# Expert slots by rank, wide and narrow in turns, and four weight pieces of the first expert in places of their own

## The chip, the cores and the metric

The kernel runs on one NeuronCore of one Trainium2 chip. The metric is the device time of one execution in microseconds (us). Engines are named as in the profile: PE is TensorE, DVE VectorE, ACT ScalarE, POOL GpSimd, and SP the SyncE queue, which issues the weight transfers.

## The reference

Two decoder blocks run one after the other on 256 tokens of width 1024, all in fp32, each with two layers of attention and feed-forward networks. The change touches one part: the second layer of the first block has, where the first layer has a dense network, a mixture of eight experts. Each token goes to its two best experts, and each expert is a gated network of width 3584:

```python
def _swiglu(x, w1, w3, w2):
    return (jax.nn.silu(x @ w1) * (x @ w3)) @ w2

def _moe(x, w_router, w1, w3, w2):
    ...
    logits = (xt @ w_router).astype(jnp.float32)
    top_v, top_e = lax.top_k(logits, TOP_K)          # TOP_K = 2, N_EXPERTS = 8
    gates = jax.nn.softmax(top_v, axis=-1)
    ...
    yb = lax.map(run, (buf.reshape(n_blocks, EXPERT_BLOCK, D), block_e)).reshape(P, D)
    y = jnp.zeros((T, D), x.dtype).at[stok].add(yb[dest] * sg[:, None].astype(x.dtype))
```

256 tokens with two experts each make 512 pairs, 64 per expert on average. For the inputs that `setup_inputs()` draws, the eight experts get 64, 73, 69, 66, 78, 76, 45 and 41 tokens.

## The kernel before

**Weights.** The weights of one expert (w1, w3 and w2, 42 MB) lie in DRAM as 28 pieces of 128 columns of its hidden width. A piece is 1536 KB, 12 KB in each of the 128 partitions: w1, w3 and w2 of these columns, a third each. The weight ring in SBUF (`weight_ring`) has room for eight pieces in this stage; seven places are used (`ROUND` = 7, `expert_unit(q)` gives place q), the eighth is empty. An expert is computed in four rounds of seven pieces (`ROUNDS` = 4).

**SP.** SP waits until PE has used up the piece in a place and then issues the next transfer into it (`load_expert`; `expert_used` counts used pieces over the whole stage). All weight transfers go through SP's one queue in program order. The first seven pieces are issued while the stage before still computes, as soon as the ring's places come free. Which expert comes first is fixed (expert 0), so that its weights can be fetched before the router has decided; the others come in order of falling token count, read from `expert_order`.

**Slots.** Each expert works on a fixed number of token slots. PE gathers the tokens into slots by a product with a 0/1 matrix (`gather`). The widths go by position in the order (`TIERS`): the first expert 88, the second 96, the other six 80, together 664. If an expert has more tokens than its position has slots, all engines take the other branch (`If(most <= CAP)`), in which each expert works on all 256 tokens.

**PE.** For a piece, `chosen_up` makes the two products with w1 and w3 and `chosen_down` the one with w2. The weights are the stationary operand and the slots the moving one; the 128 output columns are split into two strips of 64 (`GROUPS`), which run beside one another in the array. In the profile one piece is 64 matmuls at L844 (up) and 32 at L854 (down). `expert_rounds` puts down(q-1) behind up(q): a round is up 0, up 1, down 0, up 2, down 1 and so on to up 6, down 5, down 6. ACT (silu, L1448) and DVE (product, L1875) work between up and down of a piece. When an expert is done, `expert_result` turns its rows around (L861, L866) and scatters them to the tokens (L876); in the first expert the next one's gather (L819) stands between L866 and L876, in the others behind L876.

**Code.** Each of the three tiers has code of its own on PE, ACT and DVE, and the six experts of the last tier run through the same code in a loop. A round is a loop too: one pass of it holds 672 matmuls and as many weight loads.

The positions are made on DVE (L2245 to L2262): `places` is each expert's rank by token count, expert 0 always first, and comparing it with the numbers 0 to 7 gives the order.

## Time and profile before

| | us |
|---|---|
| median of three runs | 3165.56 (3163.49 to 3168.33) |
| span of the profiled execution | 3164.2 |
| expert stage, first product of the first expert to last product of the last | 859.4 to 1705.1 |
| PE busy, whole span | 3109.1 (98%) |
| transfers of expert pieces | 224 of 1536 KB |

The profiled execution's own time is its span, 3164.2 us; the median lies 1.4 us above it. The eight experts begin at 859.4, 972.4, 1093.5, 1199.1, 1301.3, 1403.5, 1506.7 and 1610.0 us. A window over one expert shows what each engine was busy with and how fast the weights came in; the chain of work shows when each round began, and where a transfer stands in the chain, PE waited for it. A busy PE is not by itself the limit: weights that come late stretch the same work.

### The profile page before, as it was taken

The numbers are of one execution on the slowest core, as the hardware profiler recorded it, in microseconds if no ns is written. First come the engines' busy times: TensorE is split into PE (matmuls) and PEld (weight loads), VectorE is DVE, ScalarE is ACT, GpSimd is POOL, SyncE is SP. The second block draws the span as 40 slices with busy tenths as digits, with TensorE's granted clock in tenths as the row PEclk, the third lists the DMA queues.
The fourth block names the chain that finished last, engine by engine and source line by source line (L and its number), as shares of the span: only waits on it lengthen the run. The fifth ranks groups of instructions, "written<-read, shape, count | busy, mean of one in ns | idle before, by whom it ended". The sixth has DMA issues, their size and how long they took to land.

```text
span 3164.2 us, 79565 instructions
## 1 busy us (share of the span) xinstructions
PE 3109.1 (98%) x36280; PEld 2651.8 (84%) x36280; DVE 1330.7 (42%) x2668; ACT 398.3 (13%) x1040; POOL 53.6 (2%) x86
## 2 busy tenths in 40 slices
PE   9999999999999999999998999999999999999998
PEld 6686894978599999999998976999895976999894
DVE  2252566543201101111013565654566575655465
ACT  1240000042110000000001001111100001121100
POOL 0000000000000000000000000000000000000000
PEclk9999999999999999999999999999999999999999
DMA  7434443433499999999997444434444444534442
GB/s 257 145 111 159 160 173 142 175 133 117 198 411 365 364 418 421 426 426 426 427 426 316 172 167 159 175 134 160 160 160 169 164 170 156 188 120 163 154 176 86
DMA packets 63109, 714.37 MB, mean 226 GB/s; under 512 B 7568, under 2 KB 9232, under 8 KB 11888
## 3 DMA queue, kind: packets, MB, share of 16 engines
q1 hardware_dynamic: 59328, 703.62, 56.5%
q0 software_dynamic: 1008, 5.94, 0.5%
q10 hardware_dynamic: 2624, 2.65, 0.4%
q8 instruction: 114, 1.87, 0.2%
q14 instruction: 35, 0.29, 0.0%
HBM read 709.30 MB, written 1.05 MB: 224 GB/s over the span
## 4 chain that ended last, share of the span: by engine, by line
PE 94%; DMA 2%; DVE 2%; ACT 1%; issue 1%; POOL 0%; SPq 0%; POOLq 0%; DVEq 0%; ACTq 0%
PE psum L653 50%; PE psum L844 15%; PE psum L774 10%; PE psum L854 8%; PE psum L912 5%; DMA weight_ring<-in_experts 2%; PE psum L1256 1%; PE psum L876 1%; PE psum L819 1%; PE psum L691 1%; PE psum L687 1%; PE psum L983 1%; PE psum L686 0%; PE psum L1230 0%; POOL statistics L575 0%
## 5 line engine op out<-in xcount | busy, mean ns | idle before, releaser
L653 PE MATMUL psum<-arena,weight_ring 128*128 128x128 f32 (+1 forms) x6752 | 938.7, 299 | 5.1 <-issue 3.2
L653 PEld LDWEIGHTS psum<-arena,weight_ring 128*128 128x128 f32 x6752 | 881.8, 192 | 49.1 <-issue 11.1
L844 PE MATMUL psum<-arena,weight_ring 128*64 128x80 f32 (+2 forms) x14336 | 553.4, 235 | 7.8 <-ACT arena L1461 6.4
L844 PEld LDWEIGHTS psum<-arena,weight_ring 128*64 128x64 f32 x14336 | 532.2, 137 | 11.6 <-ACT arena L1461 6.4
L653 PE MATMUL psum<-weight_ring,arena 128*128 128x128 f32 (+4 forms) x3264 | 494.8, 309 | 2.7 <-DVE arena L2069 2.7
L653 PEld LDWEIGHTS psum<-weight_ring,arena 128*128 128x128 f32 x3264 | 431.7, 192 | 55.2 <-issue 34.2
L1875 DVE TENSOR_TENSOR arena<-arena,psum 128x80 f32<-128x80 f32 (+2 forms) x224 | 54.0, 241 | 716.6 <-ACT arena L1448 716.6
L854 PE MATMUL psum<-arena,weight_ring 128*64 128x80 f32 (+2 forms) x7168 | 296.5, 235 | 5.4 <-issue 5.3
L854 PEld LDWEIGHTS psum<-arena,weight_ring 128*64 128x64 f32 x7168 | 276.5, 137 | 6.4 <-issue 6.4
L912 PE MATMUL psum<-weight_ring,arena 128*128 128x512 f32 x384 | 166.9, 593 | 0.0
L912 PEld LDWEIGHTS psum<-weight_ring,arena 128*128 128x128 f32 x384 | 72.3, 190 | 86.1 <-issue 86.0
L1448 ACT ACTIVATE arena<-psum 128x80 f32<-128x80 f32 (+2 forms) x224 | 53.7, 240 | 712.3 <-PE psum L844 712.3
L653 PE MATMUL psum<-arena 128*128 128x128 f32 (+3 forms) x1072 | 135.8, 279 | 0.0
L774 PE MATMUL psum<-weight_ring,arena 128*128 128x512 f32 x270 | 135.5, 593 | 0.0
L1764 DVE TENSOR_TENSOR weight_ring<-weight_ring,psum 128x256 f32<-128x256 f32 x50 | 21.1, 422 | 259.5 <-ACT weight_ring L1435 259.5
L653 PEld LDWEIGHTS psum<-arena 128*128 128x128 f32 (+1 forms) x1072 | 126.3, 186 | 2.1 <-issue 1.0
L774 PE MATMUL psum<-weight_ring 128*128 128x512 f32 x260 | 125.5, 593 | 0.0
L774 PEld LDWEIGHTS psum<-weight_ring 128*128 128x128 f32 x260 | 49.5, 190 | 62.1 <-issue 62.1
L774 PEld LDWEIGHTS psum<-weight_ring,arena 128*128 128x128 f32 x270 | 50.7, 190 | 60.2 <-issue 60.2
L653 PE MATMUL psum<-weight_ring 128*128 128x128 f32 x800 | 97.5, 275 | 0.0
L653 PEld LDWEIGHTS psum<-weight_ring 128*128 128x128 f32 x800 | 93.4, 192 | 0.0
L774 PE MATMUL psum<-arena,weight_ring 128*128 128x512 f32 x180 | 86.2, 592 | 0.0
(289 smaller groups left out, 2286.8 us busy)
## 6 DMA issues: line engine op xcount, KB each, us to landing
weight_ring<-in_experts SPq DMA_DIRECT2D x224, 1536.0 KB, 12.0
weight_ring<-in_ffn_up SPq DMA_DIRECT2D x44, 2048.0 KB, 7.7
weight_ring<-in_second_wide SPq DMA_DIRECT2D x42, 2048.0 KB, 7.8
weight_ring<-in_first_wide SPq DMA_DIRECT2D x35, 2048.0 KB, 7.9
weight_ring<-in_ffn_down SPq DMA_DIRECT2D x20, 2048.0 KB, 7.7
weight_ring<-in_dense_up SPq DMA_DIRECT2D x11, 2048.0 KB, 7.7
weight_ring<-in_dense_down SPq DMA_DIRECT2D x5, 2048.0 KB, 7.7
weight_ring<-in_ffn_down SPq DMA_DIRECT2D x4, 1024.0 KB, 4.9
```

Of the source, the lines that this page charges most:

```text
L653: m = pe.matmul(o, lhs, rhs, start=i == 0, stop=i == len(terms) - 1)
L687: return pe.matmul(o[:, P:MAP], q[:, P:SEQ], k, start=True, stop=True)
L691: m = pe.transpose(o[:, n * P:(n + 1) * P], weights[:, n * P:(n + 1) * P], ident[:])
L774: return pe.matmul(psum[:, bank], lhs, rhs, start=p == 0, stop=p == FFN_STEPS - 1, skip_group_check=True)
L819: mm = pe.matmul(psum[g * STRIP:(g + 1) * STRIP, 6 + k // 4, k % 4 * CAP:k % 4 * CAP + tokens], X[:, h, at:at + STRIP], slots_hot[:, h, 0: ...
L844: mm = pe.matmul(psum[g * STRIP:(g + 1) * STRIP, q % 4, m * CAP:m * CAP + tokens], w[:, m, k, g * STRIP:(g + 1) * STRIP], chosen[:, k, 0:t ...
L854: mm = pe.matmul(psum[g * STRIP:(g + 1) * STRIP, 4 + k // 4, k % 4 * CAP:k % 4 * CAP + tokens], w[:, at:at + STRIP], hT[:, q % 4, 0:tokens ...
L876: m = pe.matmul(psum[:, 2 + 2 * h + n], tokens_hot[0:CAP, h, :], expert_rows[0:CAP, n * 512:(n + 1) * 512], start=True, stop=True)
L912: m = pe.matmul(banks(jobs, name)[:, n, :], lhs[:, k, half * P:(half + 1) * P], w[:, k, :], start=k == 0, stop=k == KT - 1, skip_group_che ...
L983: m = pe.matmul(banks(J, "latent0")[:, h, :], xT[:, k, h * P:(h + 1) * P], w[:, k, :], start=k == 0, stop=k == KT - 1, skip_group_check=True)
L1448: nc.scalar.activation(sil[:, q % 2, 0:tokens], psum[:, q % 4, 0:tokens], ACT.Silu).then_inc(moe["silu"].sem, 1)
L1875: v.tensor_tensor(hT[:, q % 4, 0:tokens], sil[:, q % 2, 0:tokens], psum[:, q % 4, apart:apart + tokens], ALU.mult).then_inc(moe["gated"].s ...
```

## The change

Four things change.

- The widths no longer fall with the position. `SLOTS_AT` gives 80, 64, 72, 88, 72, 80, 96 and 64 slots to the eight positions, together 616, and `RANK_AT` says which rank by token count stands at each position: the first is still expert 0, then the rank 7 (fewest tokens), 5, 2, 4, 3, 1 (most tokens) and 6. DVE compares `places` with this table instead of with 0 to 7.
- The tiers are gone: every position has code of its own on PE, ACT and DVE, and every expert but the last gathers for the next one between L866 and L876 (line numbers of before).
- The last four pieces of the first expert (24 to 27) get places of their own (`kept_units`): two in the arena at 28 and 72 KB and one in three parts at 84, 51 and 55 KB, free at that time, and one in the eighth place of the ring. SP fetches the first two behind a wait for the second attention branch's product in layer 1, the third behind the fourth piece of the ring and a wait for the embedding's projection, the fourth behind the seventh piece. They come as twelve transfers of 512 KB.
- So the first expert's last round fetches only three pieces through the ring (`RUNNING` = 3), and has its own copy of the code on PE. The four places left over get the second expert's pieces 3 to 6, which SP issues ahead of its pieces 0 to 2.

```diff
-TIERS = ((0, MIDDLE, MIDDLE_CAP, CAP), (MIDDLE, FULL, CAP, SMALL_CAP), (FULL, EXPERTS, SMALL_CAP, SMALL_CAP))
+RANK_AT = (0, 7, 5, 2, 4, 3, 1, 6)
+SLOTS_AT = (80, 64, 72, 88, 72, 80, 96, 64)
+KEPT = 4
+RUNNING = ROUND - KEPT
...
+        kept_units = [thirds(view(28, EXPERT_UNIT)), thirds(view(72, EXPERT_UNIT)),
+                      [view(kb, KT * P) for kb in (84, 51, 55)], thirds(expert_unit(ROUND))]
...
+            def keep(j):
+
+                at = (EXPERT_UNITS - KEPT + j) * P
+                for n, part in enumerate(kept_units[j]):
+                    sp.dma_start(part, a["experts"][at:at + P, n * KT * P:(n + 1) * KT * P]).then_inc(kept_loaded, 16)
...
+                    if l == 1 and u == MIX1 - 1:
+
+                        sp.wait_ge(*f["full"].by(1, JOBS1[1]["branch_b1"] + 1))
+                        for j in range(2):
+                            keep(j)
...
+                if q == 3:
+                    sp.wait_ge(*f["full"].by(1, JOBS1[1]["ple_proj1"] + 1))
+                    keep(2)
+            keep(3)
...
-            with sp.Fori(1, ROUNDS) as g:
+            with sp.Fori(1, ROUNDS - 1) as g:
                 load_expert(0, g, 0)
+            load_expert(0, ROUNDS - 1, 0, range(RUNNING))
             sp.wait_ge(*once["slotted"].by(0))
             for r in range(1, EXPERTS):
                 expert = sp.value_load(expert_order[0:1, r:r + 1], min_val=0, max_val=EXPERTS - 1)
-                with sp.Fori(0, ROUNDS) as g:
+                if r == 1:
+                    for q in range(RUNNING, ROUND):
+                        sp.wait_ge(expert_used, ROUND * (ROUNDS - 2) + q + 1)
+                        load_unit(q, 0, expert)
+                    load_expert(1, 0, expert, range(RUNNING))
+                with sp.Fori(1 if r == 1 else 0, ROUNDS) as g:
                     load_expert(r, g, expert)
...
+                            if last_of_first and q >= RUNNING:
+                                pe.wait_ge(kept_loaded, 16 * 3 * KEPT)
...
-                        for first, last, tokens, following in TIERS:
-                            with pe.Fori(first, last) as e:
-                                if first == FULL:
-                                    gather(e, tokens)
-                                expert_rounds(e, lambda q: chosen_up(q, tokens), lambda q: chosen_down(q, tokens), route["columns"])
-                                expert_result(e, following if last < FULL else None)
+                        for e, tokens in enumerate(SLOTS_AT):
+                            expert_rounds(e, lambda q, parts: chosen_up(q, parts, tokens), lambda q, parts: chosen_down(q, parts, tokens), route["columns"])
+                            expert_result(e, SLOTS_AT[e + 1] if e + 1 < EXPERTS else None)
...
-                    v.tensor_tensor(placed, places.unsqueeze(1).broadcast_to(square), iota.unsqueeze(2).broadcast_to(square), ALU.is_equal).then_inc(once["slotted"].sem, 1)
+                    v.tensor_tensor(placed, places.unsqueeze(1).broadcast_to(square), ranks.unsqueeze(2).broadcast_to(square), ALU.is_equal).then_inc(once["slotted"].sem, 1)
```

On SP, the row of weight transfers from the last pieces of attention to the expert stage's first loop stands like this before. Transfers into `arena` and `weight_ring` are named by what they read, and the row in brackets is what SP waits for first:

```order
L490 DMA weight_ring<-in_first_wide 128x4096 [waits unit_used] x9
L490 DMA weight_ring<-in_ple_proj 128x2048 [waits unit_used]
L490 DMA weight_ring<-in_first_wide 128x4096 [waits unit_used] x2
L528 DMA weight_ring<-in_experts 128x3072 [waits unit_used] x7
L535 UNCONDITIONAL_BRANCH
```

And after the change, at the same place:

```order
L497 DMA weight_ring<-in_first_wide 128x4096 [waits unit_used] x9
L511 DMA arena<-in_experts 128x1024 [waits first_full]
L511 DMA arena<-in_experts 128x1024 x5
L497 DMA weight_ring<-in_ple_proj 128x2048 [waits unit_used]
L497 DMA weight_ring<-in_first_wide 128x4096 [waits unit_used] x2
L546 DMA weight_ring<-in_experts 128x3072 [waits unit_used] x4
L511 DMA arena<-in_experts 128x1024 [waits first_full]
L511 DMA arena<-in_experts 128x1024 x2
L546 DMA weight_ring<-in_experts 128x3072 [waits unit_used] x3
L511 DMA weight_ring<-in_experts 128x1024 x3
```

Twelve transfers have come in, at three points of the same queue, two of them behind waits for PE (`first_full`).

On PE, the end of the second expert and the start of the loop over the other six stands like this before (L861 and L866 turn results, L876 scatters, L819 gathers):

```order
L861 MATMUL psum<-identity,arena 96x128 x2
L866 MATMUL psum<-identity,arena 96x128 x8
L876 MATMUL psum<-arena 128x512 x4
L1198 REGISTER_ALU
L1198 COMPARE_AND_BRANCH
L1198 UNCONDITIONAL_BRANCH
L1198 ISA
L819 MATMUL psum<-arena,x_rows 64x80 x32
L825 UNCONDITIONAL_BRANCH
L825 ISA
L830 REGISTER_ALU
L844 MATMUL psum<-arena,weight_ring 64x80 x64
```

And at the same place after the change, from the second expert's end to the third's first products (L910 and L915 turn, L852 gathers, L925 scatters, L893 is up):

```order
L910 MATMUL psum<-identity,arena 96x128 x2
L915 MATMUL psum<-identity,arena 96x128 x8
L852 MATMUL psum<-arena,x_rows 64x72 x32
L925 MATMUL psum<-arena 128x512 x4
L880 UNCONDITIONAL_BRANCH
L880 ISA
L893 MATMUL psum<-arena,weight_ring 64x72 x64
```

The loop over experts is gone, the gather stands ahead of the scatter, and the third expert's products are 72 wide.

## Rows read from the trace of the kernel before

**Rows 1.** The page: span, and the chain that ended last, by line.

```profile
span 3164.2 us, 79565 instructions
...
PE psum L653 50%; PE psum L844 15%; PE psum L774 10%; PE psum L854 8%; PE psum L912 5%; DMA weight_ring<-in_experts 2%; PE psum L1256 1%; PE psum L876 1%; PE psum L819 1%; PE psum L691 1%; PE psum L687 1%; PE psum L983 1%; PE psum L686 0%; PE psum L1230 0%; POOL statistics L575 0%
```

**Rows 2.** Windows, first, third and fifth expert (us; busy per engine; PEclk, DMA, GB/s).

```profile
859.41:972.42 113.01, 110.83 (x2772) 107.45 (x2774) 10.23 (x35) 13.67 (x35) 0.00 (x0) 1.00 0.97 398
...
1093.45:1199.11 105.66, 101.53 (x2771) 98.18 (x2771) 12.11 (x38) 8.50 (x31) 0.00 (x0) 1.00 0.94 389
...
1301.33:1403.51 102.18, 100.75 (x2770) 97.81 (x2770) 12.12 (x38) 8.49 (x31) 0.00 (x0) 1.00 1.01 426
```

**Rows 3.** Chain by time, rounds' first pieces, experts one to four: start, us, what.

```profile
859.41 5.07 PE psum L844 x128
887.91 4.85 PE psum L844 x128
913.39 4.85 PE psum L844 x128
...
972.42 5.43 PE psum L844 x128
1001.45 5.20 PE psum L844 x126
1029.17 5.20 PE psum L844 x126
...
1093.45 4.65 PE psum L844 x128
1120.29 4.54 PE psum L844 x128
1143.64 4.47 PE psum L844 x128
...
1199.11 4.65 PE psum L844 x128
1222.57 4.46 PE psum L844 x128
```

**Rows 4.** Chain by time, last pieces of the last three experts: issue, us to landing.

```profile
1473.74 19.34 DMA weight_ring<-in_experts
...
1576.87 19.53 DMA weight_ring<-in_experts
...
1680.21 20.18 DMA weight_ring<-in_experts
...
1702.87 2.24 PE psum L854 x64
```

**Rows 5.** Timeline, PE, the router's product: 8 columns against 128 weight columns.

```profile
834.98 3.64 PE L653 MATMUL psum<-arena 128*128 128x8 f32 x32
```

**Rows 6.** Timeline, PE, from the first expert's end to the second's start.

```profile
964.28 0.43 PE L861 MATMUL psum<-identity,arena 128*96 128x128 f32 x2
...
965.93 2.86 PE L819 MATMUL psum<-arena,x_rows 128*64 128x96 f32 x64
...
972.35 5.50 PE L844 MATMUL psum<-arena,weight_ring 128*64 128x96 f32 x128
```

**Rows 7.** Timeline, PE, two waits in the third expert's first round.

```profile
1113.66 0.78 PE L854 MATMUL psum<-arena,weight_ring 128*64 128x80 f32 x17 [1.52 <-issue]
...
1119.43 0.85 PE L854 MATMUL psum<-arena,weight_ring 128*64 128x80 f32 x18 [1.14 <-issue]
```

**Rows 8.** DMA queues, third expert's window: packets, MB, share (PE's code).

```profile
q8 instruction: 6, 0.10, 0.3%
```

**Rows 9.** Timeline, SP: the first refill of the ring and those behind it.

```profile
866.74 93.28 SPq L533 DMA_DIRECT2D weight_ring<-in_experts  x26
```

**Rows 10.** DMA issues, window 866.3 to 867.5: one piece alone, us to landing.

```profile
weight_ring<-in_experts SPq DMA_DIRECT2D x1, 1536.0 KB, 6.2
```

**Rows 11.** Windows, the third expert's first 6 us (columns as in rows 2).

```profile
1093.45:1099.50 6.05, 6.05 (x174) 6.05 (x176) 0.47 (x2) 0.47 (x2) 0.00 (x0) 1.00 0.04 16
```

More of the change, by code:

```diff
@@ L299, in build @@
         pT = view(56, 2 * SEQ, "p (k t) -> p k t", k=2)
-        router = view(60, KT * EXPERTS + EXPERTS + 3 * P + 2 * EXPERTS)
+        router = view(60, KT * EXPERTS + EXPERTS + 3 * P + 3 * EXPERTS)
         chosen = view(0, KT * CAP, "p (k t) -> p k t", k=KT)
@@ L835, in expert_rounds, with unit_parts, chosen_up @@
                             pe.wait_ge(*moe["gated"].by(e, ROUND * g + q))
-                            down(q - 1).then_inc(expert_used, 1)
-            def chosen_up(q, tokens):
-                w = expert_unit(q)[:, 0:EXPERT_UP].rearrange("p (m k n) -> p m k n", m=2, k=KT)
+                            down(q - 1, unit_parts(q - 1, last_of_first)).then_inc(expert_used, 1)
+                if isinstance(e, int) and e == 0:
+                    with pe.Fori(0, ROUNDS - 1) as g:
+                        one_round(g)
+                    one_round(ROUNDS - 1, True)
+                else:
+                    with pe.Fori(0, ROUNDS) as g:
+                        one_round(g)
+            def unit_parts(q, last_of_first):
+                return kept_units[q - RUNNING] if last_of_first and q >= RUNNING else thirds(expert_unit(q))
+            def chosen_up(q, parts, tokens):
+                w = [part.rearrange("p (k n) -> p k n", k=KT) for part in parts[0:2]]
                 for m in range(2):
@@ L877, in expert_result, with whole_up, whole_down @@
                     m.then_inc(route["scattered"].sem, 1)
-            def whole_up(q):
-                w = expert_unit(q)[:, 0:EXPERT_UP].rearrange("p (m k n) -> p m k n", m=2, k=KT)
+            def whole_up(q, parts):
+                w = [part.rearrange("p (k n) -> p k n", k=KT) for part in parts[0:2]]
                 for m in range(2):
-                    mm = product([(psum[:, q % 4, m * SEQ:(m + 1) * SEQ], w[:, m, k], xT[:, k, :]) for k in range(KT)])
+                    mm = product([(psum[:, q % 4, m * SEQ:(m + 1) * SEQ], w[m][:, k], xT[:, k, :]) for k in range(KT)])
                 return mm
-            def whole_down(q):
-                w = expert_unit(q)[:, EXPERT_UP:]
+            def whole_down(q, parts):
+                w = parts[2]
                 for h in range(HALVES):
@@ L1583, in _ @@
                         gathered_columns(0)
-                        for first, last, tokens, _ in TIERS:
-                            with act.Fori(first, last) as e:
-                                if first == FULL:
-                                    gathered_columns(e)
-                                expert_silus(e, tokens)
-                                expert_result(e, last < FULL)
+                        for e, tokens in enumerate(SLOTS_AT):
+                            expert_silus(e, tokens)
+                            expert_result(e, e + 1 < EXPERTS)
                     with act.Else():
@@ L2278, in _ @@
                     with dve.If(most <= CAP):
-                        for first, last, tokens, _ in TIERS:
-                            with dve.Fori(first, min(last, EXPERTS - 1)) as e:
-                                clear_accumulators(4 * CAP, 2)
-                                expert_tiles(e, tokens, CAP)
-                                expert_result(e)
-                        clear_accumulators(4 * CAP, 2)
-                        expert_tiles(EXPERTS - 1, SMALL_CAP, CAP)
-                        expert_result(EXPERTS - 1, first_half)
+                        for e, tokens in enumerate(SLOTS_AT):
+                            clear_accumulators(4 * CAP, 2)
+                            expert_tiles(e, tokens, CAP)
+                            expert_result(e, first_half if e + 1 == EXPERTS else None)
                     with dve.Else():
@@ L2676, in arrange @@
                                repeated(np.append([2.0 * SEQ], np.arange(EXPERTS - 2, -1, -1) / EXPERTS).astype(np.float32)),
-                               repeated(np.repeat([float(CAP - tokens) for _, _, tokens, _ in TIERS], [last - first for first, last, _, _ in TIERS]).astype(np.float32))], axis=1),
+                               repeated(np.array([CAP - tokens for tokens in SLOTS_AT], np.float32)), repeated(np.array(RANK_AT, np.float32))], axis=1),
         lambdas=np.concatenate([repeated(i[n][l]) for l in range(LAYERS) for n in ("lambda_q1", "lambda_k1", "lambda_q2", "lambda_k2")], axis=1),
```

35 lines of the change are left out of this document (19 added, 16 removed).

## Prediction

> **What bounds the kernel now.** The page comes first: the span is 3164.2 us, and its chain is PE nearly everywhere; the one transfer in it is that of the expert weights, 2% [rows 1]. So I read the expert stage alone, 859.4 to 1705.1 us, where all of the change lies but three early transfers. The windows by expert [rows 2] are to show two regimes. In the first expert (88 slots) PE is busy for 110.8 of 113.0 us and the weights come at 398 GB/s; in the fifth (80 slots) they come at 426 GB/s, DMA share 1.01.
>
> Next the price of a piece on either side. On PE: from one round's start to the next are 25.48 us with 88 slots (887.91 to 913.39), 27.72 with 96, 23.35 with 80 [rows 3]; by seven, 3.64, 3.96 and 3.33 us a piece, or 0.04 us per slot and piece. In the queue: the last pieces of experts six to eight landed at 1493.08, 1596.40 and 1700.39 [rows 4]; 103.32 us for 28 pieces is 3.69 us each (the last expert took 0.7 more). At 80 slots PE is thus faster than the queue inside the rounds and gives it back in the 9 us between experts: 102.2 against 103.3 us per expert, a balance. The two wide experts are PE's (113.0 and 121.0 us from start to start), and after them the full ring lets the queue stand: 16 GB/s in the third expert's first 6 us [rows 11]. So neither fewer slots alone nor an earlier queue alone is worth its own sum; I go through the stage expert by expert and take at each the later of the two.
>
> **The change part by part.**
>
> *Widths.* 664 slots become 616: 48 x 28 x 0.04 = 54 us of matmul less on PE, if the line goes on below 80. 72 slots then cost 3.01 us a piece. For 64 the nearest bound is the router's product [rows 5]: it moves 8 columns against 128 weight columns and still takes 3.64/32 = 0.114 us, the price of loading. A strip has half as many weight columns, 0.057 us; two strips load beside each other (at 80 slots a matmul starts every 3.33/96 = 0.035 us, which excludes one after the other), so 48 pairs take 2.73 us. The line says 2.69; I take 2.73. Per expert: 76.4 us (64), 84.2 (72), 93.3 (80), 101.9 (88), 110.9 (96).
>
> *Between experts.* The first expert's order, gather between turning and scatter, now holds for all: 964.28 to 972.35 is 8.1 us with a 96-wide gather of 2.86 in it [rows 6]. Narrower gathers scale: 7.1 us ahead of 64 slots, 7.2 (72), 7.4 (80), 7.7 (88), 8.1 (96). The loop's experts pay 102.2 - 4 x 23.35 = 8.8.
>
> *Code.* Eight positions have code of their own instead of three, and the first expert's last round a further copy. A first reading is not free: the first rounds took 28.50, 29.03 and 26.84 us, 3.0, 1.3 and 3.5 over the next ones, while the fourth expert, second through the loop, took 23.46 [rows 3]. The waits are PE's own [rows 7], and six code packets of 16 KB came in that window [rows 8], so one feeds about 128 matmuls. After a wait PE resumed at 1113.66 and again at 1119.43: 5.77 us per packet, for 128 x 0.035 = 4.4 us of work. A late packet costs 1.3 us at 80 slots, so 3.5 us are 2.6 late ones; at 64 a late one costs 2.1, at 72 1.8. I take 6 us (64), 5 (72), 3.5 (80, twice in the first expert), 3.0 (88), 1.3 (96). This is the least certain term: zero is one end, all five later packets late the other (10.6 us at 64).
> Of this the Trainium skill (Runtime: NRT & Kernel Launch, Instruction fetch mechanics) says that the sequencer fetches the next 16 KiB block while it executes the current one, so that crossing a boundary is mostly hidden; by it this term is zero, and the total is the first rival's. The trace has 1.3 to 3.5 us per first reading and disagrees.
>
> *Kept pieces.* The first two are issued behind the second branch's product, before the projection's weights, so that two pieces (7.4 us) stand ahead of these in the queue while PE has the mixing products left; the third follows the ring's fourth piece, the fourth its seventh, when the queue has nothing else. What SP then waits for was computed before the next load could start, so nothing queued behind is late: cost nothing. If that cover failed, the most is these 7.4 us. What they bring is settled by the ring. In the first expert the queue's first refill goes out at 866.74 [rows 9] and lands 6.2 us later [rows 10]. It has 17 pieces of this expert and seven of the next to bring: 872.9 + 23 x 3.69 = 957.8. Then all places are full until the second expert's first piece is used.
>
> **The sum.** Start 859.4 as before.
> First (80): 93.3 + 3.5 + 3.5 + 7.1; the second starts at 966.8.
> Second (64): its first piece is used two ups and a down later (5/3 x 2.73 = 4.6), at 971.4, and the refill lands at 977.6. The queue has stood for 16 us, longer than the four kept pieces' 14.8: their lead is lost. 20 more pieces: 1051.4. PE alone would end at 966.8 + 76.4 + 6 = 1049.2; it waits and ends 3.6 us after the last landing (up, down, down), 1055.0. Next start 1062.2.
> Third (72): queue 1051.4 + 103.3 = 1154.7, PE's end 4.0 later, 1158.7 (alone 1151.4). Next start 1166.4.
> Fourth (88): PE 101.9 + 3.0, end 1271.3 (queue 1258.0). Next 1278.5.
> Fifth (72): PE 1367.7, queue 1361.3 + 4.0: PE by 2 us. Next 1375.1.
> Sixth (80): PE 1471.9, queue 1464.6 + 4.4: PE by 3. Next 1480.0.
> Seventh (96): PE 1592.2; the ring runs full. Next 1599.3.
> Eighth (64): seven pieces ahead, then again the refill rule: 1599.3 + 4.6 + 6.2 + 20 x 3.69 = 1683.9, end 3.6 later: 1687.5 (PE alone 1681.7).
> Code packets share the queue; the last expert of before lost 0.7 us somewhere, and I add 1.5: 1689. Before, the last product ends at 1705.1 [rows 4]. What follows stays. Gain 16 us: the profiled execution, 3164.2 us, becomes 3148, and the median of the runs, 1.4 us above it, 3149.5.
>
> **The rivals.**
> *Code reading hides.* All first-reading losses zero: the same steps give the second's start at 959.8, the fourth's at 1159.4, then the queue in the fifth and sixth, the eighth's start at 1588.1, and 1677 at the end: 28 us gained, 3137.5. For it: wherever PE waits for weights anyhow a loss costs nothing. Against: the losses that [rows 3] show, and the fourth to seventh experts, where PE sets the time and nothing hides one. The Trainium skill's page named above would have it so. 0.15.
> *The kept lead pays in full.* The queue does not stop after the first expert, 14.8 us more ahead: then PE sets every expert but the last, end 1676, 3136.5. Against: there is no place to load into. 0.05.
> *Narrow products don't pay.* If 64 and 72 slots run at the 3.33 us of 80, PE sets all experts: second's start 966.8, then 1070.8, 1175.3, 1287.4, 1391.6, 1496.5, 1615.8, end 1712.6: 7.5 us slower, 3173. It decides from about 3.2 us a piece at 64. For it: no row below 80. Against: [rows 5]. 0.08.
> *Code waits behind a full queue.* The three first readings of before fell into windows slower than 426 GB/s (398 and 389 in the first and third [rows 2]), with pauses [rows 11]; now the queue pauses only after the first expert. If a packet's turn grows from 5.8 to about 9 us, the losses are 2.5 times mine: 15 us at 64, 12.5 at 72, 8.75 at 80, 7.5 at 88. PE then sets nearly every expert, end near 1726: 21 us slower, 3186. The result turns to slower than before at 1.85 times my losses, a turn of some 7.4 us. For it: already in the sixth to eighth experts the last piece took 19 to 20 us from issue to landing [rows 4], against 6.2 alone. Against: PE's waits slow the refills too, which empties the queue. 0.10 for over 1.5 times.
> *The counts don't fit.* Then the other branch runs, with 256 columns where now there are 80 to 96, more than twice the stage. By rank 78, 76, 73, 69, 66, 45, 41 tokens meet 96, 88, 80, 72, 72, 64, 64 slots, expert 0's 64 meet 80: under 0.01.
>
> **How the numbers follow.** The forecast, 3143 to 3157 with the first-reading term between half and 1.4 times mine, has 0.55; the rest, 0.06, is what I have not thought of, spread evenly. 0.2% is 6.3 us, about what a measurement of this kernel tells from no change: under 3159.2 is faster. The forecast, the two first rivals and a little of the rest give 0.77. Same, 3159 to 3172, takes half of the narrow rival, the milder half of the full-queue rival and some rest: 0.13. Slower is 0.10. The range 3136 to 3166 takes in the two fast rivals' ends and the code losses up to 1.7 times; the narrow and the full-queue rival's far ends stay out.
>
> **What would show it.** Rounds of 18.8 to 19.6 us at 64 slots and 21.0 at 72; a near zero rate at about 958 to 972 us; waits of PE for weights in the second, third and eighth experts and hardly any in the fourth to seventh; first rounds longer than the next by 1 to 6 us, most at 64. Wrong would be: no pause of the queue after the first expert, PE waits named "issue" of over 60 us in all, or narrow rounds near 23 us.

## The result, and the profile after

The changed kernel takes 3175.2 us (median of five runs, 3169.6 to 3184.2) against 3165.6: 1.0032 times the time before, 95% interval 1.0021 to 1.0042. It is slower by 0.3%, where 0.5% faster was forecast; the time lies outside the range. The profiled execution took 3169.6 us, the fastest of the five; its span is 3167.8 us, 3.6 over that of before.

The page of the changed kernel (PE busy; the chain that ended last, by engine and by line; the queue of code packets), to be read against [rows 1]:

```profile
span 3167.8 us, 79420 instructions
...
PE 3075.1 (97%) x36280; PEld 2613.5 (83%) x36280; DVE 1328.5 (42%) x2668; ACT 397.6 (13%) x1040; POOL 53.7 (2%) x86
...
q8 instruction: 150, 2.46, 0.3%
...
PE 92%; DMA 4%; DVE 2%; issue 2%; ACT 1%; POOL 0%; SPq 0%; POOLq 0%; DVEq 0%; ACTq 0%
PE psum L686 49%; PE psum L893 13%; PE psum L807 10%; PE psum L903 7%; PE psum L961 5%; DMA weight_ring<-in_experts 4%; PE psum L1303 1%; PE psum L925 1%; PE psum L852 1%; PE psum L724 1%; PE psum L720 1%; PE psum L1032 1%; PE psum L719 0%; POOL statistics L608 0%; PE psum L1277 0%
```

PE is busy for 34 us less than before (3075.1 against 3109.1) and the span is 3.6 us longer. The waits have taken all of it, and the share of the weight transfers in the chain has gone from 2% to 4%. Lines 893 and 903 are now up and down, 925 scatters.

Windows of the changed kernel, expert by expert and then the whole stage (us; busy time of PE, PEld, DVE, ACT and POOL; PEclk, DMA share, GB/s), and the whole stage of the kernel before:

```profile
859.70:970.90 111.20, 103.58 (x2770) 99.91 (x2770) 10.00 (x35) 13.54 (x35) 0.00 (x0) 0.98 0.90 369
970.90:1071.30 100.40, 89.58 (x2773) 85.40 (x2772) 11.58 (x38) 8.13 (x31) 0.00 (x0) 0.98 0.93 387
1071.30:1175.60 104.30, 95.27 (x2771) 91.32 (x2770) 11.87 (x38) 8.33 (x31) 0.00 (x0) 0.98 1.01 423
1175.60:1289.70 114.10, 110.27 (x2771) 106.79 (x2770) 12.34 (x38) 8.74 (x31) 0.00 (x0) 1.00 1.00 421
1289.70:1390.40 100.70, 95.02 (x2771) 91.24 (x2770) 11.86 (x38) 8.34 (x31) 0.00 (x0) 0.98 0.97 401
1390.40:1498.20 107.80, 101.95 (x2771) 98.49 (x2770) 12.10 (x38) 8.52 (x31) 0.00 (x0) 1.00 1.01 424
1498.20:1617.30 119.10, 118.30 (x2771) 115.40 (x2770) 12.58 (x38) 8.89 (x31) 0.00 (x0) 1.00 0.99 395
1617.30:1710.10 92.80, 83.15 (x2690) 81.39 (x2690) 8.24 (x31) 6.27 (x28) 0.00 (x0) 0.98 0.89 366
859.70:1710.10 850.40, 797.11 (x22079) 769.94 (x22080) 90.57 (x294) 70.76 (x249) 0.00 (x0) 0.99 0.96 399
```

```profile
859.40:1705.10 845.70, 830.10 (x22079) 806.55 (x22080) 92.15 (x294) 71.67 (x249) 0.00 (x0) 1.00 0.98 406
```

In the stage PE is busy for 33.0 us less (830.1 to 797.1) and waits 37.7 us more (15.6 to 53.3).

The windows show one thing more: before, the granted clock (PEclk) was 1.00 over the stage, and now it is 0.98 in five experts. In the second, third, fifth and eighth there is one short stretch each at half the granted clock (1.2 in place of 2.4 GHz), in the first round, beside the end of that round's longest wait, 2.3 to 2.5 us named "issue". In the first expert the clock was already at half when the stage began. A window over the fifth expert's stretch, and two rows of the chain, 64 matmuls each, before it and in it:

```profile
1310.70:1314.10 3.40, 3.40 (x64) 3.40 (x61) 0.00 (x0) 0.00 (x0) 0.00 (x0) 0.50 0.89 345
```

```profile
1305.05 2.01 PE psum L893 x64
1310.67 3.63 PE psum L893 x64
```

This one cost PE 1.6 us, and it counts as busy time: part of the 797.1 us is the same work done more slowly.

What PE waits for, in the changed kernel and then before (us in total, times, longest):

```profile
PE psum L893 <- issue: 18.6, 13, 2.5
PE psum L903 <- issue: 17.0, 12, 2.4
PE psum L893 <- DMA weight_ring<-in_experts: 15.8, 25, 1.5
```

```profile
PE psum L854 <- issue: 5.3, 5, 1.5
...
PE psum L844 <- DMA weight_ring<-in_experts: 0.6, 4, 0.2
```

"Issue", time in which PE waits for nothing that the profile shows, has grown by 30.3 us, and the waits for weights by 15.2. The timeline of PE in the first expert's last round shows how issue time comes about (start, busy time, line, operation, wait before it):

```profile
948.88 2.36 PE L893 MATMUL psum<-arena 128*64 128x80 f32 x62 [1.56 <-issue]
...
955.08 1.25 PE L893 MATMUL psum<-arena 128*64 128x80 f32 x30 [1.56 <-issue]
...
961.28 1.25 PE L903 MATMUL psum<-arena 128*64 128x80 f32 x30 [1.55 <-issue]
```

PE resumes every 6.20 us, and between two of these rows the trace has exactly 128 matmuls, which need 4.4 us. In the trace's records of q8, the queue that brings PE's code, the packets lie in step with it: one starts at 952.63 and one at 958.75, each 3.7 us after PE resumed, takes 1.0 us, and PE goes on 1.4 to 1.5 us after its end. So a turn, from one resumption of PE to the next, is 3.7 + 1.0 + 1.5 us, and the largest part is the time before the packet starts. When the packet was asked for the trace does not show. A piece takes the weight queue 3.69 us.

### The profile page after: what moved, and what is told of

It reads as the page before. It is cut to its first block, busy times and chain, and to the rows that moved or that the text cites. A ratio compares the mean times of both kernels' runs of the same rounds, so it can differ in the third digit from the quotient of the medians.

```text
span 3167.8 us, 79420 instructions
## 1 busy us (share of the span) xinstructions
PE 3075.1 (97%) x36280; PEld 2613.5 (83%) x36280; DVE 1328.5 (42%) x2668; ACT 397.6 (13%) x1040; POOL 53.7 (2%) x86
## 4 chain that ended last, share of the span: by engine, by line
PE 92%; DMA 4%; DVE 2%; issue 2%; ACT 1%; POOL 0%; SPq 0%; POOLq 0%; DVEq 0%; ACTq 0%
PE psum L686 49%; PE psum L893 13%; PE psum L807 10%; PE psum L903 7%; PE psum L961 5%; DMA weight_ring<-in_experts 4%; PE psum L1303 1%; PE psum L925 1%; PE psum L852 1%; PE psum L724 1%; PE psum L720 1%; PE psum L1032 1%; PE psum L719 0%; POOL statistics L608 0%; PE psum L1277 0%
## 5 line engine op out<-in xcount | busy, mean ns | idle before, releaser
L893 PE MATMUL psum<-arena,weight_ring 128*64 128x80 f32 (+4 forms) x14144 | 524.9, 232 | 32.3 <-DMA weight_ring<-in_experts 15.8
L893 PEld LDWEIGHTS psum<-arena,weight_ring 128*64 128x64 f32 x14144 | 503.4, 138 | 43.0 <-issue 23.6
L1919 DVE TENSOR_TENSOR arena<-arena,psum 128x80 f32<-128x80 f32 (+4 forms) x224 | 52.6, 235 | 714.6 <-ACT arena L1495 714.4
L903 PE MATMUL psum<-arena,weight_ring 128*64 128x80 f32 (+4 forms) x7072 | 283.0, 232 | 15.7 <-issue 15.5
L903 PEld LDWEIGHTS psum<-arena,weight_ring 128*64 128x64 f32 x7072 | 263.5, 139 | 17.6 <-issue 17.5
L1495 ACT ACTIVATE arena<-psum 128x80 f32<-128x80 f32 (+4 forms) x224 | 52.7, 235 | 742.1 <-PE psum L893 742.1
L1808 DVE TENSOR_TENSOR weight_ring<-weight_ring,psum 128x256 f32<-128x256 f32 x50 | 21.1, 421 | 259.8 <-ACT weight_ring L1482 259.8
```

Source lines behind the costliest of these rows:

```text
L893: mm = pe.matmul(psum[g * STRIP:(g + 1) * STRIP, q % 4, m * CAP:m * CAP + tokens], w[m][:, k, g * STRIP:(g + 1) * STRIP], chosen[:, k, 0:t ...
L903: mm = pe.matmul(psum[g * STRIP:(g + 1) * STRIP, 4 + k // 4, k % 4 * CAP:k % 4 * CAP + tokens], w[:, at:at + STRIP], hT[:, q % 4, 0:tokens ...
L1495: nc.scalar.activation(sil[:, q % 2, 0:tokens], psum[:, q % 4, 0:tokens], ACT.Silu).then_inc(moe["silu"].sem, 1)
L1919: v.tensor_tensor(hT[:, q % 4, 0:tokens], sil[:, q % 2, 0:tokens], psum[:, q % 4, apart:apart + tokens], ALU.mult).then_inc(moe["gated"].s ...
```

## Experiments

Theory: the narrower products are worth what their durations say, but reading eight copies of code while the weight queue is busy takes it back, since each packet of code waits behind weights under way. Rivals: the kept pieces, the order or the narrow products are at fault, or the reading itself is slow whatever the queue does. The kernel before had a median of 3165.6 to 3167.3 us beside all of these runs. Some profiles begin the stage 3 to 4 us later than others (in these the granted clock was at half from about 838 to 844 us, ahead of the stage), so that lengths of the stage are compared, not ends. The columns "stage" and "PE <- issue" (waits of PE put down to issue in the stage) are of the one profiled execution.

| kernel | median, us | to before | stage, us | PE <- issue, us |
|---|---|---|---|---|
| before | 3167 | 1 | 845.7 | 5.3 |
| changed | 3175.2 | 1.0032 | 850.4 | 35.6 |
| before, eight copies | 3187.8 | 1.0064 | 862.0 | 22.0 |
| changed, no kept pieces | 3165.9 | 0.9999 | 846.1 | 33.3 |
| the same, own copy of the fourth round | 3173.5 | 1.0021 | 851.7 | 37.8 |
| the same, rising widths | 3174.9 | 1.0024 | 852.9 | 42.0 |
| changed, pieces in thirds | 3191.3 | 1.0080 | 869.4 | 44.3 |
| changed, two thirds of the weights | 3116.2 | 0.9834 | 796.6 | 13.7 |
| changed, one third of the weights | 3106.2 | 0.9806 | 784.6 | 3.6 |
| all 80 slots, one loop | 3139.2 | 0.9915 | 818.0 | 3.2 |
| all 80 slots, eight copies | 3171.1 | 1.0008 | 847.4 | 29.3 |
| loops of 80 and of 72 | 3143.7 | 0.9923 | 820.9 | 9.1 |
| loop of 80, last 96 | 3158.7 | 0.9974 | 838.4 | 5.0 |

### Copies of code alone

```diff
-TIERS = ((0, MIDDLE, MIDDLE_CAP, CAP), (MIDDLE, FULL, CAP, SMALL_CAP), (FULL, EXPERTS, SMALL_CAP, SMALL_CAP))
+TIERS = ((0, MIDDLE, MIDDLE_CAP, CAP), (MIDDLE, FULL, CAP, SMALL_CAP), *((n, n + 1, SMALL_CAP, SMALL_CAP) for n in range(FULL, EXPERTS)))
```

> The kernel before with one edit: the six experts that share one loop of 80 slots get six copies of the loop's body, so that TensorE reads new code five times more; widths, order and weight transfers are those of before. Theory (the code that is read while the weight queue is busy is what the change paid): each of the five further copies loses TensorE 5 to 6.5 us, as the first reading of an 80-slot copy did in the changed kernel's first and sixth expert (5.0 and 6.5 us), 25 to 32 us in all; of these some 4 us are hidden by the waits for weights that the last three experts already have (rounds of 24.39, 24.59 and 25.24 us against 23.27), so the time is 3186 to 3194 us, and q8 has some 30 packets more. Rival A (the change's slowness comes from the kept pieces, the order or the narrow products, not from code): 3163 to 3169 us. Rival B (the two outer copies already showed the price, 1.06 us at 96 slots and 3.43 us at 80): five times 3.4 us, 3176 to 3182 us.

Measured 3187.8 us, 1.0064 (1.0050 to 1.0077), +20.7 us. The waits of PE in the stage of this kernel:

```profile
PE psum L854 <- issue: 12.8, 13, 1.7
PE psum L844 <- issue: 9.2, 9, 1.9
```

22.0 us where there were 5.3. Nothing but the number of copies differs: code alone costs 20.7 us for five copies, 4.1 each. The five copies' first rounds took 26.5, 27.1, 29.0, 27.7 and 26.7 us against 23.2 for the next ones, 3.3 to 5.7 too many. Rival A is out. Between the theory and rival B, 3.4 us each, the run does not decide as well: the median lies in the theory's range, but the profiled execution is the fastest of the five (3182.1 us), and its stage has grown by 16.3 us, 3.3 a copy.

### Without the kept pieces

```diff
-                    if l == 1 and u == MIX1 - 1:
...
-                        for j in range(2):
-                            keep(j)
...
-            with sp.Fori(1, ROUNDS - 1) as g:
+            with sp.Fori(1, ROUNDS) as g:
                 load_expert(0, g, 0)
-            load_expert(0, ROUNDS - 1, 0, range(RUNNING))
```

> The changed kernel without the four kept weight pieces: the slots by rank, the widths in turns and the eight copies stay; the weight transfers and the first expert's four rounds in one loop are those of before. Theory (the kept pieces' lead is given back in the 16.7 us pause of the weight queue after the first expert, while the code of the first expert's last round, which has a copy of its own only because of them, costs some 5.8 us): the two cancel to a few us, 3168 to 3180 us. Rival A (the lead is worth what the four pieces take in the queue, 4 x 3.69 = 14.8 us, and a worse kernel would be seen without it): 3184 to 3194 us. Rival B (the kept pieces are what makes the change slow): at or under 3160 us.

Measured 3165.9 us, 0.9999 (0.9990 to 1.0008): no difference from before, 9.3 us faster than the change. This lies under the range of the theory, a miss: the kept pieces do not come out even, they cost. Slots, turns and copies alone come out even. With the kept pieces the extra copy of the first expert's last round is gone too; what of the 9.3 us is that copy the next run tells.

### A copy of code for the first expert's fourth round, no kept pieces

The edit is to the kernel of the run above.

```diff
-                with pe.Fori(0, ROUNDS) as g:
-                    one_round(g)
+                if isinstance(e, int) and e == 0:
+                    with pe.Fori(0, ROUNDS - 1) as g:
+                        one_round(g)
+                    one_round(ROUNDS - 1)
+                else:
+                    with pe.Fori(0, ROUNDS) as g:
+                        one_round(g)
```

> The changed kernel without kept pieces (3165.9 us) and with one edit: the first expert's fourth round gets a copy of the code of its own, as in the changed kernel. Theory (what the kept pieces cost is this copy's reading, 5.8 us in the round of 29.28 against 23.41 us): 3170 to 3175 us, so that most of the 9.3 us between the changed kernel and the one without kept pieces is code. Rival (it is the twelve early transfers or the 16.7 us pause of the queue): 3164 to 3168 us.

Measured 3173.5 us (3170.6 to 3180.1), +7.6 against 3165.9. The first expert's window without the copy, and then with it:

```profile
859.40:964.80 105.40, 101.09 (x2772) 97.76 (x2772) 9.97 (x35) 13.48 (x35) 0.00 (x0) 1.00 0.96 397
```

```profile
862.60:974.80 112.20, 102.18 (x2772) 98.17 (x2772) 10.01 (x35) 13.47 (x35) 0.00 (x0) 1.00 0.97 401
```

6.8 us more in this one expert, for the same work, as the theory expected. The copy, which the change needs only because the kept pieces lie elsewhere, is 7.6 of the 9.3 us. The other 1.7 us, the kept transfers themselves, is less than the runs scatter; no gain from them is to be seen.

### Pieces in thirds

```diff
+PARTS = [slice(n * KT * P, (n + 1) * KT * P) for n in range(3)]
...
-                sp.dma_start(expert_unit(q), a["experts"][bass.ds((expert * EXPERT_UNITS + ROUND * g + q) * P, P), :]).then_inc(expert_loaded[q], 16)
+                for part in PARTS:
+                    sp.dma_start(expert_unit(q)[:, part], a["experts"][bass.ds((expert * EXPERT_UNITS + ROUND * g + q) * P, P), part]).then_inc(expert_loaded[q], 16)
```

> The changed kernel with one edit: each 1536 KB weight piece of the experts is fetched by three transfers of 512 KB, its two up parts and its down part, in place of one; TensorE still waits for all three. Theory (a code packet waits behind the share of one whole transfer on its DMA engine, 3.66 to 3.75 us of the 6.2 us that 128 matmuls take in a stall): the share is a third, 1.23 us, so a turn is 1.2 + 1.05 + 1.45 = 3.7 us, which is below what 128 matmuls take at 72 slots and more (2.73 to 3.96 us for 96 gives 3.6 us at 64 and 4.4 us at 80); the losses of some 50 us fall to under 15, and the queue becomes the bound: 3133 to 3150 us. Rival A (the 6.2 us are the reading itself and not the wait behind a transfer): 3168 to 3182 us, with turns of 6.2 us as before. Rival B (transfers a third as long cost the queue more than 3.69 us a piece): above 3182 us.

Measured 3191.3 us, 1.0080 (1.0066 to 1.0094): the theory in this form fell, and of the rivals A has the turn and B the time. The same stretch of PE's timeline as above, and the window of the third expert:

```profile
954.51 2.36 PE L896 MATMUL psum<-arena 128*64 128x80 f32 x62 [1.56 <-issue]
...
960.71 1.26 PE L896 MATMUL psum<-arena 128*64 128x80 f32 x30 [1.56 <-issue]
...
966.90 1.26 PE L906 MATMUL psum<-arena 128*64 128x80 f32 x30 [1.55 <-issue]
```

```profile
1079.90:1188.20 108.30, 96.05 (x2771) 91.61 (x2770) 11.86 (x38) 8.33 (x31) 0.00 (x0) 0.98 1.03 409
```

The turn is still 6.20 us. And at a DMA share of 1.03 the queue brings 409 GB/s where whole pieces come at 423 to 426, 3.85 us a piece. So the packet does not wait for the rest of one transfer: three transfers that are issued together hold it up as one does. That left two readings, the bytes under way or the reading itself.

### Fewer bytes in the queue

Two kernels leave out a part of every piece that comes through the ring later on; their products run on what lies in the ring from its first filling.

```diff
-                sp.dma_start(expert_unit(q), a["experts"][bass.ds((expert * EXPERT_UNITS + ROUND * g + q) * P, P), :]).then_inc(expert_loaded[q], 16)
+                sp.dma_start(expert_unit(q)[:, 0:EXPERT_UP], a["experts"][bass.ds((expert * EXPERT_UNITS + ROUND * g + q) * P, P), 0:EXPERT_UP]).then_inc(expert_loaded[q], 16)
```

> The changed kernel, but every later piece in the ring is fetched without its down part (1024 of 1536 KB; the down products read what the ring's first filling left there), so that a piece takes the queue some 2.46 us in place of 3.69 and the queue is no bound; code, slots, order and kept pieces are untouched. The changed kernel's rounds without any loss add up to an end of the last product at some 1636 us against 1710. Theory (a code packet waits behind what the queue still has under way, 3.7 us of the turn of 6.2; thirds of a piece left the turn at 6.2 because the three thirds are under way together): the wait falls to 2.5 us or less, the turn to 5 us or less, the losses from some 50 us to 10 to 25, the end to 1646 to 1661 and the time to 3110 to 3127 us. Rival (the turn of 6.2 us is the reading itself): losses of some 50 us stay, 3148 to 3156 us.

Measured 3116.2 us, 0.9834. The second run fetched `0:KT * P` in place of `0:EXPERT_UP`:

> The changed kernel, but every later piece in the ring is fetched with its first up part alone (512 of 1536 KB; the other products read what the ring's first filling left), 1.23 us of the queue for a piece. With two parts of three (2.46 us) the turn of 128 matmuls fell from 6.2 to 5.1 and 5.6 us and the losses on code from some 50 to some 18 us (3116.2 us). Theory (a code packet waits behind what the weight queue has under way): the wait falls to 1.2 us and the turn to 1.2 + 1.0 + 1.45 = 3.7 us, about what 128 matmuls of 64 slots take (3.6 us), so hardly a stall is left: losses of 3 to 9 us, 3100 to 3110 us. Rival (what is left at two thirds is the reading itself): 3113 to 3118 us, as with two thirds.

Measured 3106.2 us, 0.9806. PE's waits in the stage with two thirds of the weights, and two stalls of the second expert from its timeline:

```profile
PE psum L893 <- issue: 7.6, 6, 2.1
PE psum L903 <- issue: 6.1, 6, 1.8
```

```profile
978.62 1.74 PE L893 MATMUL psum<-arena,weight_ring 128*64 128x64 f32 x53 [1.42 <-issue]
...
983.71 0.85 PE L893 MATMUL psum<-arena,weight_ring 128*64 128x64 f32 x21 [1.14 <-issue]
```

And with one third:

```profile
PE psum L903 <- issue: 2.9, 4, 1.2
...
PE psum L893 <- issue: 0.7, 2, 0.5
```

Code, copies and products are those of the change; only the bytes in the weight queue differ. The turn falls from 6.2 to 5.1 us with two thirds, where packets start 1.4 to 2.8 us after PE resumed, and with one third hardly a stall is left. Issue time in the stage goes 35.6, 13.7, 3.6 us, and neither kernel has a stretch at half clock in the stage. Both times lie in the theory's ranges: the price of a first reading is set by how busy the weight queue is. The last run also bounds the worth of the narrow products: with hardly any code or weights late the stage takes 784.6 us, 66 less than in the change and 61 less than before. With all the weights that is out of reach, since the queue needs 103.3 us an expert, 826 in all.

### One loop of 80 slots, and eight copies of it

```diff
-FULL = 2
-MIDDLE = 1
-MIDDLE_CAP = 11 * SEQ * 2 // EXPERTS // 8
-TIERS = ((0, MIDDLE, MIDDLE_CAP, CAP), (MIDDLE, FULL, CAP, SMALL_CAP), (FULL, EXPERTS, SMALL_CAP, SMALL_CAP))
+FULL = 0
+TIERS = ((0, EXPERTS, SMALL_CAP, SMALL_CAP),)
```

> The kernel before with all eight experts at 80 slots in one loop, so that their code is read once; no kept pieces, the order of before. The largest expert then has room for 80 tokens in place of 96 (with more, the kernel takes its other branch); with these inputs the largest has 78. Theory (width is worth what the matmuls' durations say, and code is what costs): the first expert 113.0 -> 106 to 108 us, the second 121.1 -> 102 to 103 us, the other six 102 to 103.3 us each, where the queue's 28 x 3.69 = 103.3 us is the limit; the end comes 21 to 27 us earlier, 3138 to 3146 us. Rival A (the queue is the bound in any case and narrower experts only move its waits): 3155 to 3166 us. Rival B (only the alternation of small and large widths can use a narrower expert): the same, at or above 3155 us.

Measured 3139.2 us, 0.9915 (0.9901 to 0.9929), as the theory expected, 28 us faster than before and 36 us faster than the change. The fifth expert's window:

```profile
1273.30:1376.60 103.30, 101.48 (x2772) 98.05 (x2772) 12.07 (x38) 14.92 (x37) 0.00 (x0) 1.00 1.01 426
```

PE and the queue are in balance (101.5 us busy, 426 GB/s). The second kernel has `TIERS = tuple((n, n + 1, SMALL_CAP, SMALL_CAP) for n in range(EXPERTS))`:

> The kernel with eight experts of 80 slots, with eight copies of the loop's body in place of one loop (3139.2 us); slots, order and weight transfers are the same. Theory (each copy's code is read at 4 to 6 us while the weight queue is busy; 6 us of waits for weights at the ends of the last five experts hide a part): seven further copies cost 22 to 36 us, 3161 to 3175 us. Rival (the gain of the one loop over the kernel before, 28 us, is width alone and the copies cost little): 3139 to 3147 us.

Measured 3171.1 us, 1.0008 (0.9999 to 1.0018). Its waits:

```profile
PE psum L852 <- issue: 15.8, 15, 1.9
PE psum L842 <- issue: 13.5, 16, 1.6
```

31.9 us for seven copies, 4.6 each, as expected. That is more than the whole gain of 80 slots for all over the kernel before. The seven first rounds were 4.0 to 4.8 us too long, and 7.1 in the one of the third expert, which has a stretch at half clock.

### Narrower products in a loop

```diff
+TIERS = ((0, 4, SMALL_CAP, SMALL_CAP), (4, EXPERTS, 72, 72))
```

> The kernel with one loop of 80 slots (3139.2 us), split in two loops: four experts of 80 slots, then four of 72; the code is read twice. The 72-slot loop needs some 9 us of TensorE less for each expert. Theory (the queue is the floor at 103.3 us an expert, so a narrower product only waits): 3136 to 3142 us, the same as with 80, the waits for weights in the last four experts up by some 9 us each. Rival (a narrower expert shortens the stage by what its products save, less one reading of code): 3105 to 3115 us.

Measured 3143.7 us (3139.8 to 3146.9), 0.9923 (0.9909 to 0.9936), where 3136 to 3142 was expected. The second expert with 72 slots:

```profile
1382.70:1486.00 103.30, 94.66 (x2770) 89.76 (x2770) 11.87 (x38) 8.32 (x31) 0.00 (x0) 1.00 1.01 426
```

The length is that of the 80-slot expert to the tenth, with PE 6.8 us less busy: the queue is the floor, 28 x 3.69 us. Narrower than 80 slots brings nothing where no lead in weights has been built up. The 4.4 us over the single loop, which took the time just past the range, are about what one more reading of code costs.

### Rising widths in place of turns

```diff
-RANK_AT = (0, 7, 5, 2, 4, 3, 1, 6)
-SLOTS_AT = (80, 64, 72, 88, 72, 80, 96, 64)
+RANK_AT = (0, 7, 6, 5, 4, 3, 2, 1)
+SLOTS_AT = (80, 64, 64, 72, 72, 80, 88, 96)
```

> The changed kernel without kept pieces (3165.9 us) and with one edit: the widths rise, 80, 64, 64, 72, 72, 80, 88, 96, in place of small and large in turns; the same eight copies, the same products. Theory (the queue with 3.69 us a piece is the floor, an expert of 28 pieces needs it for 103.3 us; in turns, each wide expert leaves the queue idle and each narrow one then waits, while rising widths have the queue without a pause until the wide ones, and hide the code of the narrow ones in waits for weights): the pauses of the queue fall from some 30 us to under 12, and the end comes at 1675 to 1688 in place of 1705, 3136 to 3150 us. Rival (turns are needed, since narrow experts in a row empty the ring): at or above 3166 us.

Measured 3174.9 us, 1.0024 (1.0015 to 1.0033): wrong by some 30 us, on the rival's side. Windows of the first two 64-slot experts, the last 72-slot one and the last expert:

```profile
968.60:1070.40 101.80, 89.77 (x2771) 85.58 (x2770) 11.59 (x38) 8.13 (x31) 0.00 (x0) 0.98 1.01 420
1070.40:1175.20 104.80, 90.58 (x2773) 85.97 (x2772) 11.58 (x38) 8.14 (x31) 0.00 (x0) 0.98 1.01 424
...
1280.40:1384.40 104.00, 93.85 (x2771) 89.63 (x2770) 11.88 (x38) 8.34 (x31) 0.00 (x0) 1.00 1.01 423
...
1604.70:1716.00 111.30, 111.30 (x2691) 111.14 (x2690) 9.29 (x32) 7.09 (x29) 0.00 (x0) 1.00 0.77 308
```

The queue ran without a pause through the narrow experts, as I had expected (420 to 424 GB/s), but that gave no lead in weights: the four of them took 415.8 us in all, about the queue's full price of 413.2, and the wide ones behind them cost PE's full price while the queue ran out of work (308 GB/s in the last). In turns (the kernel without kept pieces), the 72 slots behind the 88 take 99.6 us. Taking turns is thus worth 9 us, 3174.9 against 3165.9.

### Room for the largest expert again

```diff
-TIERS = ((0, EXPERTS, SMALL_CAP, SMALL_CAP),)
+TIERS = ((0, 7, SMALL_CAP, SMALL_CAP), (7, EXPERTS, CAP, CAP))
+RANK_AT = (0, 2, 3, 4, 5, 6, 7, 1)
```

> The kernel with one loop of 80 slots, with room for the largest expert again: seven experts of 80 slots in one loop, then the expert with the most tokens in a copy of its own with 96 slots. Theory (wide products cost TensorE 28 x 0.63 = 17.6 us, 1 to 5 us of code come on top, and the queue's waits of some 1.3 us an expert's end are no longer last): the end comes at 1693 to 1698 us in place of 1677.5, 3154 to 3160 us, faster than the kernel before by 7 to 13 us. Rival (the queue, which is the floor with one loop, hides the wider products too): 3139 to 3146 us.

Measured 3158.7 us, 0.9974 (0.9964 to 0.9984), as expected. It keeps 96 slots for the expert with the most tokens and still beats both kernels, by 8.6 and 16.5 us. Where 80 slots suffice, the single loop at 3139.2 us is the better one.

## Why the prediction was wrong

The stage's last product was forecast at 1689 us and came at 1710.1. Expert by expert (start to start, the last to the end of its products):

| slots | forecast | measured | first reading, forecast | measured |
|---|---|---|---|---|
| 80 | 107.4 | 111.2 | 3.5 and 3.5 | 5.0 and 5.9 |
| 64 | 95.4 | 100.4 | 6 | 6.3 |
| 72 | 104.2 | 104.3 | 5 | 9.3 |
| 88 | 112.1 | 114.1 | 3.0 | 4.6 |
| 72 | 96.6 | 100.7 | 5 | 5.4 |
| 80 | 104.9 | 107.8 | 3.5 | 6.5 |
| 96 | 119.3 | 119.1 | 1.3 | 0.8 |
| 64 | 89.7 | 92.8 | 6 | 6.4 |

*Right: widths and the time between experts.* A round with 72 slots took 21.0 us, as forecast, and one with 64 19.65, 2.81 a piece (2.73 forecast); the step from 72 to 64 saves 0.19 a piece where the wider steps save some 0.32. PE's busy time in the stage fell by 33 us, not by the 54 forecast for the matmuls alone; with one third of the weights it is 779.2 us, 50.9 less than before, so that most of what is missing is not a matter of width: where code and weights come late the same matmuls count as busy for longer, in part at half clock. Between experts it was 7.2 to 8.0 us (7.1 to 8.1). The rival in which narrow products don't pay is out.

*Right: the kept lead is lost.* The queue was forecast to stand for 16 us after the first expert; it stood for 16.7 by its landings. The window before SP's first refill:

```profile
955.00:976.10 21.10, 19.25 (x449) 16.31 (x450) 6.30 (x14) 2.78 (x7) 0.00 (x0) 1.00 0.28 114
```

*Two steps failed. The first is the code term, mis-sized.* I took 36.8 us of first readings; they were 50.2, 1.36 times that. The 80-slot price of 3.5 us came from the third expert of before, whose first 6 us had a nearly idle queue [rows 11]; with the queue busy it was 5.0 to 6.5 here (3.3 to 5.7 in the run on copies alone), and the turn of a packet 6.2 us, not 5.8 [rows 7]. The half clock behind the waits is in these figures, and I had given it no term. Of the 21 us by which the stage's end came late, 3.8 lie in the first expert, 1.6 in the fourth and 3.0 in the sixth for this alone. My argument that PE's stalls empty the queue did not hold: it ran at 421 to 424 GB/s in the third, fourth and sixth experts. The third's 9.3 us cost nothing, as it waits for weights anyway (104.3 against 104.2), and in the seventh wide products hide code, as forecast.

*The second and larger one: late code makes weights late.* 1.36 times my losses lies inside the 1.4 for which I had forecast 3157 at most, so the code term alone does not explain the miss. In each expert I took the later of PE and a queue that runs at its undisturbed 3.69 us a piece, and gave 1.5 us to packets in the queue, in the last expert alone. The second, fifth and eighth experts, which end on their weights, came out longer by 5.0, 4.1 and 3.1 us than forecast, 12.2 of the 21. The chain of the changed kernel by time has these waits for their last weights (issue, us to landing):

```profile
1038.25 21.67 DMA weight_ring<-in_experts
```

```profile
1358.68 19.92 DMA weight_ring<-in_experts
```

```profile
1684.50 21.60 DMA weight_ring<-in_experts
```

They end at 1059.9, 1378.6 and 1706.1 us; 1051.4, 1361.3 and 1683.9 were forecast. In the second expert 4.1 us of the 8.5 are its late start, the rest is the refill, which took 7.8 us from the issue at 976.1 in place of 6.2, and pauses of about 1 us between landings beside code packets. For the fifth I had let the queue run on without a pause; after the 88-slot expert, slower than the queue, pauses between landings added up to some 6 us, and the last round waited 3.5 us for weights. The eighth repeats the second, 4.2 us in place of 1.5. Which part of a pause is the code packet's own place in the queue and which is PE's stall, no run tells apart.

*The rest.* What follows the stage took 1.4 us less than before, where I had left it as it was. And I set the median 1.4 us above the span, where it now lies 7.4 above: 21.1 - 1.4 + 6.0 is the whole miss of 25.7 us. Why the runs of the changed kernel lie 15 us apart stays open. Of the three signs that I had named for being wrong none came; none of them watched when the weights land.

*The rivals.* The one that came true in kind is code behind a full queue; not in size, since the turn was 6.2 us and not some 9. The result is slower at 1.36 times my losses, where I had put the turning point at 1.85: I had moved only PE's part of the loss, and not the weights' part. The mechanism is shown by the runs on copies alone and on fewer bytes. The rival in which code reading hides is out for this kernel. The Trainium skill (Runtime: NRT & Kernel Launch, Instruction fetch mechanics) has the crossing of a block mostly hidden: with a third of the weights the runs agree, 3.6 us in the stage, and with all of them they do not, 35.6 us. The Trainium skill's remark in the same section that kernels prefer full unrolling has its price here, 4.1 to 4.6 us a copy.

## What to carry to other kernels

Before a loop is unrolled, look at how busy the weight queue is where the new code is first read: with a full queue a copy of PE code of six packets of 16 KB cost 4 to 8 us here, and what it buys must be worth more than that on the path. Add to that what the stalls do to others: transfers that wait for PE go out later, and the granted clock can fall. Price a first reading from one that ran beside a busy queue, not from one that fell into a pause. And where PE and the queue are within a per cent of each other, fewer columns move the bound to the queue: the gain ends where the bytes say, unless wide and narrow stages alternate.

## What the runs showed of the hardware

- A packet of 16 KB of code, which feeds 128 matmuls with their weight loads, takes 1.0 us, but started 3.7 us after PE resumed while the weight queue was full, though pieces took much longer to land in a window from the third expert into the fourth (transfers, KB, median us from issue to landing):

```profile
weight_ring<-in_experts SPq DMA_DIRECT2D x29, 1536.0 KB, 13.1
```

  So the packet waits for about one piece's time, not for all that is queued. The Trainium skill (DMA: Bandwidth & Descriptors, Queues, rings and completion order) says that a DMA engine takes turns between queues and empties a packet of descriptors of one before it goes to the next. The trace agrees that the wait is bounded; that three transfers of 512 KB held it up as long as one of 1536 KB shows that the unit is not one transfer. Whether it is counted in bytes or descriptors, or whether something else that both share sets the wait, no run shows.
- The same bytes in transfers of 512 KB came at 409 GB/s in place of 423 to 426.
- The granted clock fell to half (1.2 GHz) four times in the stage of the changed kernel, each time beside the end of a first round's longest wait named "issue"; 64 matmuls of 72 slots took 3.63 us there in place of 2.01.
- Code that stood in a loop was not read again. The whole stage of the kernel with one loop of 80 slots, eight passes, has six packets (packets, MB, share), all of them in the first pass:

```profile
q8 instruction: 6, 0.10, 0.0%
```
